# Turning queries and keys inside the first projection instead of in a stage behind it

## The chip, the cores and the metric

The kernel runs on one core of one Trainium2 chip. The metric is the device time of one execution in microseconds (us); lower is better. The median of several executions is compared. The profile is one execution more, recorded by the hardware profiler.

## The reference

Two blocks of a network on 512 tokens of 1024 features, all in float32. The part that matters here is the start of the first block. 16 meta tokens are put ahead of the 512, so there are 528 positions; the rows are normalised and multiplied by `w_in`:

```python
proj = jnp.einsum('btd,dc->btc', a, w_in)
aq, ak, av, rq, rf, ri, rg = jnp.split(proj, SPLIT_POINTS, axis=-1)

def apply_rope(z, cos, sin):
    half = z.shape[-1] // 2
    rot = jnp.concatenate([-z[..., half:], z[..., :half]], axis=-1)
    return (z * cos.astype(z.dtype) + rot * sin.astype(z.dtype)).astype(z.dtype)
```

`apply_rope` is the turning by position of the queries `aq` and the keys `ak`, before the attention's scores. Each of the seven parts of `proj` has 512 columns. The second block needs a modulation vector, `mod = silu(c) @ w_ada + b_ada`, a product of one row with a 1024 x 9216 matrix; it doesn't depend on the first block, and the kernel does it beside the first projection. Behind all this come a gated scan, a layer of 16384 experts, and the second block.

## The kernel before

The code is written for each engine by hand, in blocks. All engines meet at a barrier at the end of a block, and within one they are ordered by semaphores alone. Every engine runs its own instructions strictly in order, so what stands behind a waiting instruction waits too.

**Loading** (`load_first`) fetches the tokens and small tables. **Normalising** (`norm_to_features`) makes the features, split in a high and a low part so that three fast products stand for one in float32.

**The first projection** (`first_projection`, which calls `project`) goes over 28 weight slabs of 512 KB. Slabs 0 to 15 give features: slab b holds 128 columns of the weights, and its result `t.fm[:, b, :]` (128 x 528) is made in two halves of 264, each in a PSUM bank. Blocks 0 to 3 are the queries, 4 to 7 the keys. Slabs 16 to 27 are "wide": three groups of four slabs, each group adding up five (the last group four) outputs of 128 x 512. The way of a slab:

- SP loads it into `proj_raw`, three deep, when `proj_w_low` of the slab three before is done.
- ACT rounds it to `proj_w_high` (two deep) when PE has finished the slab two before. Then ACT moves the finished outputs from PSUM.
- DVE makes `proj_w_low`, the rest (`split_low`, L408).
- PE multiplies (L149 to L151), 48 matmuls for a slab of features, 30 or 24 for a wide one. Outputs go round eight banks.

After each `split_low` DVE calls `beside_dve`: the modulation. `w_ada` comes in 96 pieces of 128 x 768 (384 KB), fetched by POOL into the ring `ada`, four deep (L563). DVE multiplies a piece by its column of c and adds it to `ada_acc` (L579). A slab has four pieces, so slabs 24 to 27 have none. POOL first clears `ada_acc` (L556) and loads the bias (L558), and behind the 96 pieces it fetches the three tables of the rotation.

**The rotation** (`rotate_first`) is a block of its own. For each of the eight feature blocks of queries and keys PE multiplies by the matrix `turn` (which swaps and negates the halves) into a bank pair (L607), DVE multiplies that by `sin` into `swung` (L616), multiplies `t.fm` by `cos` (L618) and adds the two (L620). Two bank pairs and two `swung` buffers alternate.

**Attention** (`first_attention`) needs all that, and the causal `mask`, which SP loads at the start of the rotation block. Its scores are L676, the addition of the mask L745. The gated scan behind it is the first to read `ada_acc`.

Of the kernel before, what the change touches and what calls it, by code (L numbers as in the profile page):

```python
# [18 lines left out]
ALU = mybir.AluOpType  # L19
# [3 lines left out]
P = 128  # L23
D = 1024
# [4 lines left out]
NT = NM + T  # L29
HALF = NT // 2  # L30
BANK = 512
# [5 lines left out]
AH, AHD, AV = 4, 64, 128  # L37
# [75 lines left out]
def sbuf(nc, ctx, name, shape, dtype=F32):  # L113
    return ctx.enter_context(nc.sbuf_tensor(numbered(name), shape, dtype))
# [15 lines left out]
def psum(nc, ctx, name, shape):  # L130
    return ctx.enter_context(nc.psum_tensor(numbered(name), shape, F32))
# [147 lines left out]
def load_first(core, t, dram):  # L279

    nc = core.nc
    with ExitStack() as ctx:
# [6 lines left out]
        dots, exps = core.sem("small_dots"), core.sem("small_exps")  # L289
        block = ctx.enter_context(nc.Block(no_gpsimd_drain=True))  # L290
        n_loads = 12
        c_in = core.sem("c_in")

        @block.sync
        def _(sp):
            sp.dma_start(t.c_col[:, :], dram["c_2"]).then_inc(c_in, 16)
            sp.dma_start(t.meta[:, :], dram["meta_tokens"]).then_inc(loaded, 16)
            sp.dma_start(t.x[:, :, :], dram["x"].rearrange("o (t p) d -> p (o t) d", p=P)).then_inc(loaded, 16)
            sp.dma_start(t.ident[:, :], dram["ident"]).then_inc(loaded, 16)
            sp.dma_start(t.mix_norm[:, :], dram["mix_norm_w"]).then_inc(loaded, 16)  # L300
            sp.dma_start(t.ffn_norm[:, :], dram["ffn_norm_cols"]).then_inc(loaded, 16)
            sp.dma_start(lb_in[:, :, :], dram["rec_lb_logits"]).then_inc(loaded, 16)
            for n, name in enumerate(("diff_lambda_q1", "diff_lambda_k1", "diff_lambda_q2", "diff_lambda_k2")):
                sp.dma_start(lam_in[:, n, :], dram[name].broadcast_to([P, AHD])).then_inc(loaded, 16)
            sp.dma_start(t.mixed_scale[:, 0:AH], dram["diff_subln_w"]).then_inc(loaded, 16)
            sp.dma_start(t.mixed_scale[:, AH:AH + RH], dram["rec_norm_w"]).then_inc(loaded, 16)

        @block.vector
        def _(dve):
# [126 lines left out]
            s.used(self.n)  # L436


def project(core, feat, weights, moves, beside=None, beside_dve=None, before_moves=None, beside_act=None):

    nc = core.nc
    BANKS = 8
    slabs = weights.slabs
    N = len(slabs)
    with ExitStack() as ctx:
# [11 lines left out]
        def _(pe):  # L461
            for n, slab in enumerate(slabs):
                pe.wait_ge(low.handle, low.at(n + 1))
                hi, lo = weights.parts(n)
                for (at, count), e in zip(slab.ranges, slab.outs):
# [14 lines left out]
                    if e == slab.outs[-1]:  # L480
                        last.then_inc(used.handle, 1)
                    elif closes:
                        last.then_inc(out_done.handle, 1)


        @block.scalar
# [53 lines left out]

def first_projection(core, t, dram, feat, weights, moves, rope):

    ACH, DEEP = 768, 4
    PARTS, PER_SLAB = 9 * D // ACH, 4
    with ExitStack() as ctx:
        ada = sbuf(core.nc, ctx, "ada", [P, DEEP, ACH])
        ada_in = [core.sem(f"ada_in{i}") for i in range(DEEP)]
        ada_used, acc_clear, acc_bias = core.sem("ada_used"), core.sem("acc_clear"), core.sem("acc_bias")
        N = PARTS * KC
        assert N <= PER_SLAB * weights.n  # L550

        def beside(block):
            @block.gpsimd
            def _(pool):

                pool.memset(t.ada_acc[:, :], 0.0).then_inc(acc_clear, 1)  # L556
                pool.wait_ge(acc_clear, 1)
                pool.dma_start(t.ada_acc[0:1, :], dram["b_ada_2"]).then_inc(acc_bias, 16)  # L558
                for n in range(N):
                    if n >= DEEP:  # L560
                        pool.wait_ge(ada_used, n - DEEP + 1)
                    k, part = n // PARTS, n % PARTS
                    pool.dma_start(ada[:, n % DEEP, :], dram["w_ada_2"][0, k * P:(k + 1) * P, part * ACH:(part + 1) * ACH])\  # L563
                        .then_inc(ada_in[n % DEEP], 16)
                pool.dma_start(rope.turn[:, :], dram["rope_turn"]).then_inc(rope.tables, 16)
                pool.dma_start(rope.cos[:, :], dram["rope_cos"]).then_inc(rope.tables, 16)
                pool.dma_start(rope.sin[:, :], dram["rope_sin"]).then_inc(rope.tables, 16)

        def beside_dve(dve, slab, moved):

            for n in range(PER_SLAB * slab, min(N, PER_SLAB * (slab + 1))):
                if n == 0:
                    dve.wait_ge(acc_bias, 16)
                k, part = n // PARTS, n % PARTS
# [4 lines left out]
                dve.scalar_tensor_tensor(acc, ada[:, n % DEEP, :], t.c_col[:, k:k + 1], acc, ALU.mult, ALU.add)\  # L579
                   .then_inc(ada_used, 1)  # L580

        project(core, feat, weights, moves, beside, beside_dve)


def rotate_first(core, t, dram, rope):

    nc = core.nc
    with ExitStack() as ctx:
        turn, cos, sin, tables = rope.turn, rope.cos, rope.sin, rope.tables
        swung = sbuf(nc, ctx, "swung", [P, 2, NT])  # L590
        bank = [psum(nc, ctx, f"rot_bank{i}", [P, 2, BANK]) for i in range(2)]
        turned, swung_done = [core.sem(f"rope_{n}") for n in ("turned", "swung")]
        mask_in = core.sem("mask_in")
        block = ctx.enter_context(nc.Block(no_gpsimd_drain=True))

        @block.sync
        def _(sp):
            sp.dma_start(t.mask[:, :], dram["causal"]).then_inc(mask_in, 16)

        @block.tensor  # L600
        def _(pe):
            pe.wait_ge(tables, 48)
            for b in range(2 * AH):
                if b >= 2:
                    pe.wait_ge(swung_done, b - 1)
                for half in range(2):
                    last = pe.matmul(bank[b % 2][:, half, 0:HALF], turn[:, :], t.fm[:, b, half * HALF:(half + 1) * HALF],  # L607
                                     start=True, stop=True)
                last.then_inc(turned, 1)

        @block.vector
        def _(dve):
            chain = core.chain(dve, "dve_step")
            for b in range(2 * AH):
                dve.wait_ge(turned, b + 1)
                dve.tensor_tensor(swung[:, b % 2, :].rearrange("p (a n) -> p a n", a=2), bank[b % 2][:, :, 0:HALF],  # L616
                                  sin[:, :].rearrange("p (a n) -> p a n", a=2), ALU.mult).then_inc(swung_done, 1)
                chain.link(dve.tensor_tensor(t.fm[:, b, :], t.fm[:, b, :], cos[:, :], ALU.mult))  # L618
                dve.wait_ge(swung_done, b + 1)
                chain.link(dve.tensor_tensor(t.fm[:, b, :], t.fm[:, b, :], swung[:, b % 2, :], ALU.add))  # L620


def first_attention(core, t, dram):
# [10 lines left out]
    with ExitStack() as ctx:  # L634
# [23 lines left out]
        def long(u):  # L658
            return units[u][1] == TT - 1

        def meta_turned(u):
            return over[0:NM, 2, :] if long(u) else turn_bank[0:NM, units[u][1] + 1, :]

        @block.tensor
        def _(pe):
# [2235 lines left out]
def build(nc, dram, out):  # L2901
    NAMES.clear()
    LIMIT = 229344
    with ExitStack() as ctx:
# [10 lines left out]
        with ExitStack() as first:  # L2915
# [31 lines left out]
            behind = nc.sbuf_base  # L2947
            with ExitStack() as turned:
                t.mask = sbuf(nc, turned, "mask", [P, P])
                rotate_first(core, t, dram, rope)  # L2950
                first_attention(core, t, dram)
            gated_scan(core, t, dram)

# [158 lines left out]
```

## Time and profile before

| | |
|---|---|
| median of 3 runs | 3123.35 us (3122.04 to 3127.35) |
| the profiled execution | 3135.32 us |
| its span, first to last instruction | 3133.5 us |
| mean granted TensorE clock | 0.935 of 2.4 GHz |
| PE, DVE, ACT, POOL busy | 86%, 61%, 41%, 21% |
| projection, in the trace | 38.9 to about 233 us |
| rotation, in the trace | 233.3 to 252 us |

The stages follow one another, so a share over the whole span says little of the first 8% of it. The views used are the groups of instructions, the timelines of single engines, and busy time by window. PE is the matmul engine (PEld its weight loads), DVE the vector engine, ACT the scalar engine, POOL and SP issue DMAs. An arrow in square brackets names what ended the idle time before an instruction. "DMA to landing" is the time from issue to the semaphore.

### The profile page before, as it was taken

Reading aid. Unit: us, or ns where it says so; the run is one execution under the profiler, and the core shown is the slowest. Engines: PE = TensorE matmul, PEld = TensorE weight load, DVE = VectorE, ACT = ScalarE, POOL = GpSimd, SP = SyncE. Lnnn points to the kernel's source line nnn. Section 1 sums busy time; section 2 is a strip of 40 time slices with the busy share of each in tenths; the row PEclk is TensorE's granted clock in tenths of the full one; section 3 lists DMA queues with packets and bytes.
Section 4 is the critical chain, followed back from the end, with each engine's and each line's share of the span. In section 5 each row is a group of like instructions: output and inputs, shape, how many; then the busy total and the mean of one; then the engine's idle time right before and its main releaser. Section 6 shows DMA issues by size and latency. Waiting matters only on the chain. (4 is left out here: it accounts for less than half of the span.)

```text
span 3133.5 us, 32433 instructions
## 1 busy us (share of the span) xinstructions
PE 2688.3 (86%) x11370; PEld 1823.2 (58%) x11370; DVE 1898.3 (61%) x3882; ACT 1276.2 (41%) x2760; POOL 662.1 (21%) x638
## 2 busy tenths in 40 slices
PE   5997778797889877789999998898998886889997
PEld 5974657343444322255555554697784355778886
DVE  5757745777777677777777776554645544433323
ACT  2223423444444444555666654443243254222221
POOL 2310000444443444434444434000000100000000
PEclk8996689999999999999999999899996898999999
DMA  5950014999999999999999999454220001222321
GB/s 182 328 201 1 1 54 128 373 412 405 420 420 421 408 412 421 418 411 414 419 415 414 413 418 410 155 183 141 88 69 3 36 1 61 74 94 95 101 100 61
DMA packets 131107, 750.80 MB, mean 240 GB/s; under 512 B 17296, under 2 KB 17824, under 8 KB 64624
## 3 DMA queue, kind: packets, MB, share of 16 engines
q0 software_dynamic: 81824, 575.43, 45.1%
q1 hardware_dynamic: 49120, 173.30, 15.9%
q8 instruction: 90, 1.47, 0.2%
q14 instruction: 73, 0.60, 0.1%
HBM read 746.57 MB, written 2.10 MB: 239 GB/s over the span
## 5 line engine op out<-in xcount | busy, mean ns | idle before, releaser
L1566 PE MATMUL peer_y<-rows,diag 128*128 128x512 f32 x2048 | 995.6, 613 | 176.6 <-ACT diag L1546 165.8
L1520 DVE CUSTOM_DVE_ANT_0 rows<-rows,hidden 128x1024 f32<-128x1024 f32 x512 | 627.5, 1226 | 374.0 <-DMA rows<-in_peer_table,experts 367.3
L1507 POOL DMA_INDIRECT rows<-in_peer_table,experts x512 | 582.2, 1137 | 1046.2 <-PE peer_y L1566 799.2
L1566 PEld LDWEIGHTS peer_y<-rows,diag 128*128 128x128 f32 x2048 | 362.4, 192 | 592.4 <-ACT diag L1546 302.9
L1543 ACT ACTIVATE hid<-hid 128x1 f32<-128x1 f32 x512 | 102.7, 201 | 542.2 <-DVE hid L1520 533.0
L2020 DVE TENSOR_TENSOR piece_w_low<-piece_raw,piece_w_high 128x1024 fp32r<-128x1024 f32 x132 | 160.9, 1223 | 102.2 <-ACT piece_w_high L2015 102.2
L1546 ACT ACTIVATE diag<-ident,hid 128x128 f32<-128x128 f32 x512 | 205.6, 402 | 16.7
L2015 ACT ACTIVATE piece_w_high<-piece_raw 128x1024 fp32r<-128x1024 f32 x132 | 138.6, 1052 | 109.3 <-PE u_bank L151 77.6
L2142 DVE TENSOR_TENSOR silu<-silu,u_bank 128x256 f32<-128x256 f32 (+1 forms) x44 | 24.4, 555 | 229.1 <-PE u_bank L151 229.1
L402 ACT ACTIVATE proj_w_high<-proj_raw 128x1024 fp32r<-128x1024 f32 (+2 forms) x57 | 57.7, 1014 | 245.8 <-PE proj_bank L151 245.7
L1544 ACT ACTIVATE hid<-hid,gates 128x1 f32<-128x1 f32 x512 | 150.8, 295 | 16.6
L149 PE MATMUL peer_y<-peer_feat_high,early_w_high 128*128 128x256 f32 x352 | 144.3, 410 | 1.8 <-issue 1.8
L149 PE MATMUL query_bank<-half_feat_high,query_w_high 128*128 128x256 f32 x256 | 116.3, 454 | 15.0 <-DVE query_w_low L408 15.0
L579 DVE SCALAR_TENSOR_TENSOR ada_acc<-ada,c_col,ada_acc 128x768 f32<-128x768 f32 x96 | 95.1, 1018 | 42.1 <-DMA ada<-in_w_ada 41.6
L408 DVE TENSOR_TENSOR proj_w_low<-proj_raw,proj_w_high 128x1024 fp32r<-128x1024 f32 (+2 forms) x57 | 66.1, 1166 | 78.9 <-ACT proj_w_high L402 78.8
L151 PE MATMUL peer_y<-peer_feat_high,early_w_low 128*128 128x256 f32 x352 | 98.8, 281 | 0.0
L150 PE MATMUL peer_y<-peer_feat_low,early_w_high 128*128 128x256 f32 x352 | 98.8, 281 | 0.0
L149 PE MATMUL proj_bank<-feat_high,proj_w_high 128*128 128x264 f32 x256 | 75.5, 295 | 20.2 <-DVE proj_w_low L408 13.9
L149 PEld LDWEIGHTS peer_y<-peer_feat_high,early_w_high 128*128 128x128 f32 x352 | 66.8, 190 | 30.8 <-issue 29.8
L2130 ACT ACTIVATE act_t_high<-silu 128x256 fp32r<-128x256 f32 (+1 forms) x44 | 23.2, 526 | 148.9 <-DVE silu L2142 148.9
L150 PEld LDWEIGHTS peer_y<-peer_feat_low,early_w_high 128*128 128x128 f32 x352 | 66.7, 189 | 28.0 <-issue 27.1
L1779 DVE TENSOR_TENSOR early_w_low<-early_raw,early_w_high 128x1024 fp32r<-128x1024 f32 x66 | 80.6, 1222 | 1.1
(502 smaller groups left out, 5842.8 us busy)
## 6 DMA issues: line engine op xcount, KB each, us to landing
ada<-in_w_ada POOLq DMA_DIRECT2D x96, 384.0 KB, 4.8
piece_raw<-in_ffn_w_gate SPq DMA_DIRECT2D x44, 512.0 KB, 3.5
piece_raw<-in_ffn_w_up SPq DMA_DIRECT2D x44, 512.0 KB, 4.4
piece_raw<-in_ffn_w_down SPq DMA_DIRECT2D x44, 512.0 KB, 3.5
query_raw<-in_peer_w_query SPq DMA_DIRECT2D x32, 512.0 KB, 6.2
early_raw<-in_ffn_w_gate SPq DMA_DIRECT2D x22, 512.0 KB
early_raw<-in_ffn_w_up SPq DMA_DIRECT2D x22, 512.0 KB
early_raw<-in_ffn_w_down SPq DMA_DIRECT2D x22, 512.0 KB
```

The source lines that it names most:

```text
L149: pe.matmul(out, left[0], right[0], start=start, stop=False)
L150: pe.matmul(out, left[0], right[1], start=False, stop=False)
L151: return pe.matmul(out, left[1], right[0], start=False, stop=stop)
L579: dve.scalar_tensor_tensor(acc, ada[:, n % DEEP, :], t.c_col[:, k:k + 1], acc, ALU.mult, ALU.add)\
L1507: pool.indirect_dma_start(self.rows[:, b, :], None, self.table, bass.IndirectOffsetOnAxis(ap=self.experts[:, unit % self.SETS, n % TOPK:n ...
L1520: dve.tensor_tensor_reduce(out=self.rows[:, b, 0:D], in0=self.rows[:, b, 0:D], in1=self.hidden[:, tile, :], scale=1.0, scalar=0.0, op0=ALU ...
L1543: chain.link(act.activation(self.hid[:, 1, b:b + 1], self.hid[:, 0, b:b + 1], ACT.Gelu))
L1544: chain.link(act.activation(self.hid[:, 2, b:b + 1], self.hid[:, 1, b:b + 1], ACT.Copy, scale=self.gates[:, unit % self.SETS, n % TOPK:n % ...
L1546: act.activation(self.diag[:, b, :], self.t.ident[:, :], ACT.Copy, scale=self.hid[:, 2, b:b + 1])\
L1566: last = pe.matmul(self.y[self.bank(tile)][:, c * BANK:(c + 1) * BANK], self.diag[:, b, :], self.rows[:, b, D + c * BANK:D + (c + 1) * BAN ...
L2015: act.activation(self.w.high[:, p % self.RING, :], self.raw[:, p % self.RING, :], ACT.Copy)\
L2020: dve.tensor_tensor(self.w.low[:, p % self.RING, :], self.raw[:, p % self.RING, :], self.w.high[:, p % self.RING, :].bitcast(F32), ALU.sub ...
```

## The change

The rotation stage goes. Its PE part moves into PE's projection loop by a new hook, `beside_pe`: behind slabs 3, 6, 9, ..., 24 PE turns block 0, 1, 2, ..., 7. Its DVE part moves into `beside_dve` of the slab behind: after that slab's `split_low` and ahead of its modulation pieces. There is one bank pair and one `swung`, so the projection's outputs go round six banks instead of eight. The `ada` ring is three deep instead of four. The 96 pieces are dealt out over all 28 slabs (three or four in each) instead of four in each of the first 24. The rotation's tables are fetched behind the third piece. Clearing `ada_acc` and loading the bias move into the loading block, and the load of the mask moves to the start of attention.

```diff
@@ load_first
+        acc_clear, acc_bias = core.sem("acc_clear"), core.sem("acc_bias")
...
+        @block.gpsimd
+        def _(pool):
+            pool.memset(t.ada_acc[:, :], 0.0).then_inc(acc_clear, 1)
+            pool.wait_ge(acc_clear, 1)
+            pool.dma_start(t.ada_acc[0:1, :], dram["b_ada_2"]).then_inc(acc_bias, 16)
@@ project
-    BANKS = 8
+    BANKS = banks_used
...
+                if beside_pe is not None:
+                    beside_pe(pe, n, moved)
@@ first_projection
-    ACH, DEEP = 768, 4
-    PARTS, PER_SLAB = 9 * D // ACH, 4
+    ACH, DEEP = 768, 3
+    TURN_AT = {3 * b + 3: b for b in range(2 * AH)}
+    PARTS = 9 * D // ACH
...
-                pool.memset(t.ada_acc[:, :], 0.0).then_inc(acc_clear, 1)
-                pool.wait_ge(acc_clear, 1)
-                pool.dma_start(t.ada_acc[0:1, :], dram["b_ada_2"]).then_inc(acc_bias, 16)
                 for n in range(N):
+                    if n == DEEP:
+                        pool.dma_start(rope.turn[:, :], dram["rope_turn"]).then_inc(rope.tables, 16)
+                        pool.dma_start(rope.cos[:, :], dram["rope_cos"]).then_inc(rope.tables, 16)
+                        pool.dma_start(rope.sin[:, :], dram["rope_sin"]).then_inc(rope.tables, 16)
...
+        def beside_pe(pe, slab, moved):
+            if slab in TURN_AT:
+                b = TURN_AT[slab]
+                pe.wait_ge(moved.handle, moved.at(2 * b + 2))
+                if b == 0:
+                    pe.wait_ge(rope.tables, 48)
+                else:
+                    pe.wait_ge(swung_done, b)
+                for half in range(2):
+                    last = pe.matmul(turn_bank[:, half, 0:HALF], rope.turn[:, :], t.fm[:, b, half * HALF:(half + 1) * HALF],
+                                     start=True, stop=True)
+                last.then_inc(turned, 1)
 
         def beside_dve(dve, slab, moved):
-            for n in range(PER_SLAB * slab, min(N, PER_SLAB * (slab + 1))):
+            if slab - 1 in TURN_AT:
+                chain = core.chain(dve, "dve_step")
+                b = TURN_AT[slab - 1]
+                dve.wait_ge(turned, b + 1)
+                dve.tensor_tensor(swung[:, :].rearrange("p (a n) -> p a n", a=2), turn_bank[:, :, 0:HALF],
+                                  rope.sin[:, :].rearrange("p (a n) -> p a n", a=2), ALU.mult).then_inc(swung_done, 1)
+                chain.link(dve.tensor_tensor(t.fm[:, b, :], t.fm[:, b, :], rope.cos[:, :], ALU.mult))
+                dve.wait_ge(swung_done, b + 1)
+                chain.link(dve.tensor_tensor(t.fm[:, b, :], t.fm[:, b, :], swung[:, :], ALU.add))
+
+            for n in range(N * slab // weights.n, N * (slab + 1) // weights.n):
...
-        project(core, feat, weights, moves, beside, beside_dve)
+        project(core, feat, weights, moves, beside, beside_dve, beside_pe=beside_pe, banks_used=6)
-def rotate_first(core, t, dram, rope):
...
@@ first_attention
+        @block.sync
+        def _(sp):
+            sp.dma_start(t.mask[:, :], dram["causal"]).then_inc(mask_in, 16)
@@ build
-                rotate_first(core, t, dram, rope)
```

## Rows read from the trace of the kernel before

**Rows 1.** Groups of instructions, 0 to 300 us: count, busy and mean, idle before and releaser.

```profile
L579 DVE SCALAR_TENSOR_TENSOR ada_acc<-ada,c_col,ada_acc 128x768 f32<-128x768 f32 x96 | 95.1, 1018 | 42.1 <-DMA ada<-in_w_ada 41.6
L149 PE MATMUL proj_bank<-feat_high,proj_w_high 128*128 128x264 f32 x256 | 75.5, 295 | 20.2 <-DVE proj_w_low L408 13.9 <-PEq L164 6.3
```

**Rows 2.** Windows: length, then busy PE, PEld, DVE, ACT, POOL; clock, DMA share, GB/s.

```profile
135.00:152.00 17.00, 17.00 (x141) 16.94 (x139) 13.57 (x14) 4.58 (x9) 5.95 (x12) 1.00 0.98 346
...
233.00:253.00 20.00, 10.99 (x37) 7.40 (x39) 16.25 (x24) 0.69 (x1) 0.00 (x0) 0.86 0.01 3
```

**Rows 3.** ACT's timeline in the projection: start, duration, operation.

```profile
52.67 1.06 ACT L402 ACTIVATE proj_w_high<-proj_raw 128x1024 fp32r<-128x1024 f32 x1 [4.22 <-PE proj_bank L151]
...
76.20 1.06 ACT L402 ACTIVATE proj_w_high<-proj_raw 128x1024 fp32r<-128x1024 f32 x1 [4.25 <-PE proj_bank L151]
...
146.42 1.06 ACT L402 ACTIVATE proj_w_high<-proj_raw 128x1024 fp32r<-128x1024 f32 x1 [4.23 <-PE proj_bank L151]
...
152.27 1.06 ACT L402 ACTIVATE proj_w_high<-proj_raw 128x1024 fp32r<-128x1024 f32 x1 [4.22 <-PE proj_bank L151]
...
167.10 1.06 ACT L402 ACTIVATE proj_w_high<-proj_raw 128x1024 fp32r<-128x1024 f32 x1 [5.86 <-PE proj_bank L151]
174.03 1.06 ACT L402 ACTIVATE proj_w_high<-proj_raw 128x1024 fp32r<-128x1024 f32 x1 [5.87 <-PE proj_bank L151]
...
181.91 2.04 ACT L502 ACTIVATE tm<-proj_bank 128x512 f32<-128x512 f32 x4
...
214.21 1.06 ACT L402 ACTIVATE proj_w_high<-proj_raw 128x1024 fp32r<-128x1024 f32 x1 [2.11 <-PE proj_bank L151]
219.78 1.06 ACT L402 ACTIVATE proj_w_high<-proj_raw 128x1024 fp32r<-128x1024 f32 x1 [4.51 <-PE proj_bank L151]
```

**Rows 4.** DVE's timeline: end of loading, third slab, one period of a later slab.

```profile
14.87 0.17 DVE L329 TENSOR_SCALAR one_lb<-lb 128x4 f32<-128x4 f32 x1
...
60.91 1.22 DVE L408 TENSOR_TENSOR proj_w_low<-proj_raw,proj_w_high 128x1024 fp32r<-128x1024 f32 x1
...
94.98 2.88 DVE L579 SCALAR_TENSOR_TENSOR ada_acc<-ada,c_col,ada_acc 128x768 f32<-128x768 f32 x3
99.95 1.02 DVE L579 SCALAR_TENSOR_TENSOR ada_acc<-ada,c_col,ada_acc 128x768 f32<-128x768 f32 x1 [2.09 <-DMA ada<-in_w_ada]
```

**Rows 5.** POOL's timeline: the memset, the first four pieces, one later piece.

```profile
38.92 7.79 POOL L556 MEMSET ada_acc<- 128x9216 f32 x1 [38.47 <-POOLq L164]
...
47.67 2.17 POOL L563 DMA_DIRECT2D ada<-in_w_ada  x4
...
96.29 0.54 POOL L563 DMA_DIRECT2D ada<-in_w_ada  x1 [1.53 <-DVE ada_acc L579]
```

**Rows 6.** Timeline from the rotation's start to attention's start, all engines.

```profile
233.30 5.72 PE L607 MATMUL rot_bank<-fm,turn 128*128 128x264 f32 x16 [2.52 <-PEq L449]
...
239.96 1.16 PE L607 MATMUL rot_bank<-fm,turn 128*128 128x264 f32 x4 [0.94 <-DVE swung L616]
...
241.30 0.71 DVE L616 TENSOR_TENSOR swung<-rot_bank,sin 128x528 f32<-128x528 f32 x1
...
252.36 1.76 PE L676 MATMUL score<-fm 64*128 64x144 f32 x8 [4.94 <-PEq L588]
253.65 0.30 DVE L745 TENSOR_TENSOR score<-score,mask 128x128 f32<-128x128 f32 x1 [1.89 <-PE score L676]
```

**Rows 7.** Landing times: `ada` over all, `ada` issued at 47 to 50 us, `mask`.

```profile
DMA to landing us min/median/max: 3.4/4.8/6.4
...
DMA to landing us min/median/max: 3.7/4.3/5.0
...
DMA to landing us min/median/max: 1.7/1.7/1.7
```

**Rows 8.** Two windows of slab 2; the third figure from the end is the clock.

```profile
62.00:65.00 3.00, 2.81 (x13) 2.82 (x14) 2.84 (x4) 0.00 (x0) 1.00 (x2) 0.50 0.96 328
...
67.00:69.00 2.00, 2.00 (x19) 2.00 (x18) 1.25 (x2) 0.00 (x0) 0.00 (x0) 1.00 0.98 375
```

More of the change, by code:

```diff
@@ L436, in close, with project @@
             s.used(self.n)
-def project(core, feat, weights, moves, beside=None, beside_dve=None, before_moves=None, beside_act=None):
+def project(core, feat, weights, moves, beside=None, beside_dve=None, before_moves=None, beside_act=None, beside_pe=None,
+            banks_used=8):
     nc = core.nc
-    BANKS = 8
+    BANKS = banks_used
     slabs = weights.slabs
@@ L541, in first_projection @@
 def first_projection(core, t, dram, feat, weights, moves, rope):
-    ACH, DEEP = 768, 4
-    PARTS, PER_SLAB = 9 * D // ACH, 4
+    ACH, DEEP = 768, 3
+    TURN_AT = {3 * b + 3: b for b in range(2 * AH)}
+    PARTS = 9 * D // ACH
     with ExitStack() as ctx:
         ada = sbuf(core.nc, ctx, "ada", [P, DEEP, ACH])
+        swung = sbuf(core.nc, ctx, "swung", [P, NT])
+        turn_bank = psum(core.nc, ctx, "rot_bank", [P, 2, BANK])
         ada_in = [core.sem(f"ada_in{i}") for i in range(DEEP)]
-        ada_used, acc_clear, acc_bias = core.sem("ada_used"), core.sem("acc_clear"), core.sem("acc_bias")
+        turned, swung_done = core.sem("rope_turned"), core.sem("rope_swung")
+        ada_used, acc_bias = core.sem("ada_used"), core.sem("acc_bias")
         N = PARTS * KC
-        assert N <= PER_SLAB * weights.n
         def beside(block):
@@ L564, in _ @@
                         .then_inc(ada_in[n % DEEP], 16)
-                pool.dma_start(rope.turn[:, :], dram["rope_turn"]).then_inc(rope.tables, 16)
-                pool.dma_start(rope.cos[:, :], dram["rope_cos"]).then_inc(rope.tables, 16)
-                pool.dma_start(rope.sin[:, :], dram["rope_sin"]).then_inc(rope.tables, 16)
-        def beside_dve(dve, slab, moved):
-            for n in range(PER_SLAB * slab, min(N, PER_SLAB * (slab + 1))):
+        def beside_pe(pe, slab, moved):
[10 more added lines that the diff above has]
+                last.then_inc(turned, 1)
+        def beside_dve(dve, slab, moved):
+            if slab - 1 in TURN_AT:
[8 more added lines that the diff above has]
+            for n in range(N * slab // weights.n, N * (slab + 1) // weights.n):
                 if n == 0:
@@ L580, in beside_dve @@
                    .then_inc(ada_used, 1)
-        project(core, feat, weights, moves, beside, beside_dve)
-def rotate_first(core, t, dram, rope):
[L587 to L620, printed above, removed]
+        project(core, feat, weights, moves, beside, beside_dve, beside_pe=beside_pe, banks_used=6)
 def first_attention(core, t, dram):
```

## The prediction

> **What bounds the kernel now.** I read the page first: PE is busy for 86% of the span and DVE for 61%, and the tenths show that the stages follow one another, each with a bound of its own. Nearly all the edits lie in the first 253 us, so I asked for groups of instructions, for the timeline of each engine, and for windows of that stretch. It holds the projection (28 weight slabs, 38.9 to 231 us) and the rotation (233 to 252 us). Blocks of code end at a barrier, so what is won or lost before attention moves everything behind it by the same amount, and only this stretch needs a sum.
>
> The groups say that PE's matmuls of the projection waited 13.9 us for `proj_w_low`, and that DVE's modulation pieces waited 41.6 us for their own DMAs [rows 1]. Read them together: the engine that stands still is PE, the one that holds it is DVE, and DVE is held by the ring of `ada` buffers. The windows show how near that DMA path is to full: 0.98 of the DMA time at 346 GB/s while PE and DVE both work, and against it a rotation stage in which DVE works for 16.25 of 20 us and PE for 11 [rows 2].
>
> ACT's timeline gives the pace, since each `proj_w_high` starts when PE has finished a slab. A 264-column slab takes 5.85 us where PE is free (146.42 to 152.27), a slab of five outputs 6.93 us, one of four outputs 5.57 us; but slabs 3 to 15, from 76.20 to 152.27, took 76.1 us, not 12 x 5.85 = 70.2 [rows 3]. So DVE's pace costs 5.9 us there. One period on DVE shows why: three pieces run back to back in 2.88 us, the fourth waits 2.1 us for its DMA, and only then comes the next `proj_w_low` [rows 4]. Before that, the first modulation piece can't be fetched until a memset of 7.79 us and the bias are through on POOL [rows 5]; DVE must do eight pieces before the third `proj_w_low`, which starts at 60.91 [rows 4].
>
> **The change, part by part.** I count from the profiled execution, 3135.32 us with a span of 3133.5 us.
>
> *Rotation stage removed.* From its first matmul at 233.30 to the first of attention at 252.36: 19.06 us [rows 6]. This gain is certain, and the question is what is paid back inside the projection.
>
> *Memset and bias moved into loading.* POOL had stood idle for 38.47 us before the memset [rows 5]; loading ends on DVE at 15.04 [rows 4], so 7.8 us are hidden there, and if they weren't, at most 7.8 us would come back. The pieces now start at 38.9 instead of 47.67. DVE owes six pieces, not eight, before the third `proj_w_low`. Hand count: 38.9 + 3.7 landing [rows 7] + about 1.5 for two slab loads issued at the same time = 44; first use 1 us, reissue 0.3, landing 4.3, some 1.75 us of the three rope tables queued ahead of piece 3 (0.6 MB at the 346 GB/s of [rows 2]), three more pieces 2.9: 54.3, up to 56 with the tables' own issue, where 60.91 was. Slab 3 then ends 5 us earlier. Bounds: 3.5 and 8 (PE's wait gone altogether). I take 5.0.
>
> *Eight turns put into PE's queue.* Each is two calls, four records: 1.16 us of busy PE with a pipelined tail [rows 6], about 1.04 us until the next slab can start. 8 x 1.04 = 8.3 us. What waits behind the turn on PE is the next slab. The waits of the turn itself (`moved`, `swung_done`, tables) are for work two or more slabs old and cost nothing.
>
> *Rotation on DVE.* The first operation started 1.34 us after PE's (239.96 to 241.30) [rows 6]; three operations of about 0.7 us. Counted from PE's release of the turn, 0.3 + 2.0 = 2.3 us. DVE now **waits for PE** here: behind that wait stand the slab's modulation pieces and the next `proj_w_low`, and PE waits for that. After the turn PE has one slab (5.85 us) of work. In that time DVE must do 2.3 us of rotation, the pieces, and 1.2 us of `proj_w_low`.
> With three pieces, all landed: 2.3 + 2.9 + 1.2 = 6.4, a stall of 0.55 us.
> With four pieces, the fourth must be fetched into a buffer that the first has just left, because the ring is now three deep. The trip is use 0.96 (three in 2.88) + reissue 0.29 (the piece begun at 94.98 ends at 96.00, POOL issues at 96.29 [rows 4, 5]) + landing. Landing is 3.7 to 4.3 where little is under way and 4.8 in the median now [rows 7]; with fewer pieces in flight I take 3.7 to 4.3, a trip of 5.0 to 5.5. Then 2.3 + 5.0 + 0.96 + 1.2 = 9.5 (to 10.0), a stall of 3.6 to 4.2 us.
> The even dealing gives 3, 3, 4, 3, 4, 3, 4 pieces and repeats. Turning slabs with four are 4, 13, 16 and 25. Stalls: 3.6 to 4.2 twice, 2.5 to 3.1 before slab 17 (PE has 6.93), 3.9 to 4.5 before slab 26 (PE has 5.57), 0.55 twice, none at 19 and 22. Sum 14.7 to 17.1 us.
>
> *Ring between turns.* DVE's cycle of three slabs is 2.3 + 3.43 x 5.0 to 5.5 = 19.5 to 21.2 us; PE's with its turn is 18.6, and with the mean stall above 20.8. So 0 to 0.8 us more in each of four cycles, 0 to 3; I take 1.5. In exchange the 5.9 us of today's pace are gone, since the turning cycles replace it.
>
> *Six banks.* At slabs 20 and 24 the second output needs a bank that ACT moves only after its `proj_w_high`. The first of four moves (2.04 us) is over 0.6 us after 181.91. ACT saw the slab's end at 174.03 + 6.93 = 180.96, PE had it some 0.4 us before and gets to the second output, 1.4 us of matmuls later, at about 181.9 [rows 3]. 0.6 us twice, 1.2; with slower moves up to 2.
>
> *Pieces in slabs 24 to 27.* These had none; now about 14. They hide behind PE's 5.57 us per slab (3.4 x 0.96 + 1.2 = 4.5), except for the stall already counted. If DVE ended after PE, the surplus would show behind the last slab.
>
> *Mask.* Now fetched as attention begins. It lands 1.7 us after issue [rows 7]; DVE's first operation came 1.29 us after PE's first (252.36 to 253.65) [rows 6]: +0.4 us. Attention starts right behind a busy PE, at the full clock for a moment, which I put at 0.5 us gained (bounds 0 and 2).
>
> **Sum.** -19.06 - 5.0 + 8.3 + 15.9 + 1.5 - 5.9 + 1.2 + 0.4 - 0.5 = -3.2. With the clock (below) one time in three 2 us: -2.5. Forecast 3132.8 us for the profiled execution; the median 3123.35 is 12 us lower, and I take the same difference from it: 3120.9 us. About 0.2% (6.2 us) is what a measurement can tell from no change, so the likeliest case is "within".
>
> **Where a rule speaks.** The trace lands a piece of 384 KB in 3.4 us at best and 4.8 in the median [rows 7]. The Trainium skill, "DMA: Bandwidth & Descriptors", on the fixed cost of a DMA, fits 2.0 us plus bytes over 436 GB/s, an estimate of 2.9 us for such a piece; by it the four long stalls would be some 1.1 us shorter each and the sum near -8. No row here shows so short a landing.
> PE had slab 1 behind it before 52.67 [rows 3] and waited until the third `proj_w_low` was done at 62.1 [rows 4]; then it ran at 0.50 and was at 1.00 again by 67 us [rows 8]: 1.2 GHz for about 4.4 us (an estimate), a loss of 2.2 us. The rotation stage, with gaps of 0.94 us between its turns [rows 6] and 4 us of idle PE at its end, had a mean of 0.86 [rows 2]. The new gaps of 2.5 to 4.5 us lie between. The Trainium skill, "TensorE: Matmul & The Clock Gate", on HAM oscillation, warns that DMA waits between groups of matmuls bring the lower clock again and again; by it, each long stall costs 2.2 us more, the sum becomes +5 or so, still within.
>
> **Rivals.**
> *Faster.* The ring of three suffices: landing comes down far enough, or DVE arrives with more slack than I count, and the four long stalls shrink to 0.55. Then 14.7 becomes about 3.5 and the ring term is 0: -3.2 - 12.4 - 1.5 = -17, 3106 us. For it: DMA is at 0.98 now, and demand falls from 4 to 3.43 pieces in a slab. Against it: a lone landing is still 3.4 to 3.7 us, so the fourth piece is late. It decides (over 6.2 us) once two of the four stalls are gone. Half of it gives -9.
> *Slower.* Landing stays at today's 5.0 us because weight slabs share the path. Then the trip is 6.25 us and a turn cycle lasts 2.3 + 3.43 x 6.25 = 23.7 us: 2.5 more than the 21.2 of above in each of four cycles, 1 more in the three over wide slabs (3 x 6.93 + 1.04 and a mean stall of 0.9 make 22.7). +13, net +10.5, 3134 us. It decides (over +6.2) from a landing of about 4.7. For it: 0.98 busy DMAs. Against it: most of that landing is queueing among four pieces.
> *Within.* The sum as it stands, with the clock rule or without.
>
> **Chances.** Within 0.2%: 0.42. Faster: 0.36 (full rival 0.12, part of the stalls missing 0.24). Slower: 0.22 (landing 0.14, clock plus landing 0.08). The range reaches into both: 3107 (the full rival less its tail) to 3136 (the slower rival's centre and 2 us of lower clock). The likeliest case alone spans 3117 to 3129.
>
> **What would show it.** No rotation stage, attention's first matmul near 250 us. `proj_w_low` of slab 2 starts at 54 to 56. In slabs 4, 13, 16 and 25 DVE waits once for an `ada` DMA behind three pieces, and PE waits 2.5 to 4.5 us for `proj_w_low` after it; elsewhere under 1 us. PE's waits in the projection sum to 17 to 25 us. `ada` lands in 3.7 to 4.3 us. POOL's memset lies before 10 us. It would be wrong if the waits stand in other slabs, if the median landing is 3.4 or 5, or if PE's clock falls in the gaps.

## The result, and the profile after

The change makes the kernel slightly slower: 3131.6 us in the median of 20 runs (3124.05 to 3139.91) against 3125.62 us (20 runs, 3121.5 to 3136.13), a ratio of 1.0021, interval 1.0013 to 1.0029. The forecast was 2.5 us less, 3120.9 us, with "within 0.2%" as the likeliest case and a range of 3107 to 3136. The time lies in the range but beyond the 3117 to 3129 of the likeliest case, and it moved the other way: 6.0 us more, at the edge of 0.2% (0.19% by the medians, 0.21% by the ratio).

The profiled execution alone would mislead. Its span is 3131.0 us, 2.5 us under the one before. So I split each span at attention's first vector operation, which closes the stretch that the change touches.

The timeline of the changed kernel there, the same lines as [rows 6]:

```profile
253.56 2.06 ACT L512 ACTIVATE tm_gate<-proj_bank 128x512 f32<-128x512 f32 x4 [16.58 <-PE proj_bank L151]
...
255.99 1.76 PE L676 MATMUL score<-fm 64*128 64x144 f32 x8 [2.51 <-PEq L457]
...
259.67 0.30 DVE L745 TENSOR_TENSOR score<-score,mask 128x128 f32<-128x128 f32 x1 [9.41 <-DMA mask<-in_causal]
```

The vector operation stood at 253.65 before [rows 6] and stands at 259.67 now: +6.0 us, which is also the difference of the medians. That they agree so exactly is luck: in a second trace of the changed kernel (c2, below) it stands at 261.04. The rest took 3133.5 - 253.65 = 2879.9 us in the profile before and 3131.0 - 259.67 = 2871.3 us in the one after; no edit reaches it, and over the traces of this study it lies between 2867.3 and 2879.9. All comparisons of traces below are therefore made up to that operation.

The last moves of the projection (`tm_gate`) began at 230.87 before, 253.56 now. That is 22.7 us more, where 19.06 are saved. ACT's timeline says where, to be read as [rows 3]: each line comes when PE has finished a slab, here slabs 2 to 6, 13 to 17, 25.

```profile
64.16 1.06 ACT L409 ACTIVATE proj_w_high<-proj_raw 128x1024 fp32r<-128x1024 f32 x1 [8.98 <-PE proj_bank L151]
70.28 1.06 ACT L409 ACTIVATE proj_w_high<-proj_raw 128x1024 fp32r<-128x1024 f32 x1 [4.51 <-PE proj_bank L151]
77.04 1.06 ACT L409 ACTIVATE proj_w_high<-proj_raw 128x1024 fp32r<-128x1024 f32 x1 [5.14 <-PE proj_bank L151]
87.94 1.06 ACT L409 ACTIVATE proj_w_high<-proj_raw 128x1024 fp32r<-128x1024 f32 x1 [9.28 <-PE proj_bank L151]
93.79 1.06 ACT L409 ACTIVATE proj_w_high<-proj_raw 128x1024 fp32r<-128x1024 f32 x1 [4.23 <-PE proj_bank L151]
...
142.99 1.06 ACT L409 ACTIVATE proj_w_high<-proj_raw 128x1024 fp32r<-128x1024 f32 x1 [5.14 <-PE proj_bank L151]
153.97 1.06 ACT L409 ACTIVATE proj_w_high<-proj_raw 128x1024 fp32r<-128x1024 f32 x1 [9.36 <-PE proj_bank L151]
159.82 1.06 ACT L409 ACTIVATE proj_w_high<-proj_raw 128x1024 fp32r<-128x1024 f32 x1 [4.23 <-PE proj_bank L151]
167.65 1.06 ACT L409 ACTIVATE proj_w_high<-proj_raw 128x1024 fp32r<-128x1024 f32 x1 [6.22 <-PE proj_bank L151]
178.66 1.06 ACT L409 ACTIVATE proj_w_high<-proj_raw 128x1024 fp32r<-128x1024 f32 x1 [9.95 <-PE proj_bank L151]
...
235.93 1.06 ACT L409 ACTIVATE proj_w_high<-proj_raw 128x1024 fp32r<-128x1024 f32 x1 [5.40 <-PE proj_bank L151]
```

Slab 5 took 10.90 us, slab 14 took 10.98, slab 17 took 11.01, and the last two together 17.63: with 5.85, 5.85, 6.93 and 11.1 for the same slabs where nothing holds PE, 5.1 + 5.1 + 4.1 + 6.5 = 20.8 us too long. These are the four places that the prediction names. The turn costs less than estimated: slab 4, behind a turn, took 6.76, so 0.9 us.

DVE's timeline around the first of them, as [rows 4]:

```profile
67.61 1.22 DVE L415 TENSOR_TENSOR proj_w_low<-proj_raw,proj_w_high 128x1024 fp32r<-128x1024 f32 x1
71.09 0.71 DVE L599 TENSOR_TENSOR swung<-rot_bank,sin 128x528 f32<-128x528 f32 x1 [2.26 <-PE rot_bank L590]
...
73.19 2.88 DVE L613 SCALAR_TENSOR_TENSOR ada_acc<-ada,c_col,ada_acc 128x768 f32<-128x768 f32 x3
77.95 1.02 DVE L613 SCALAR_TENSOR_TENSOR ada_acc<-ada,c_col,ada_acc 128x768 f32<-128x768 f32 x1 [1.88 <-DMA ada<-in_w_ada]
78.89 1.22 DVE L415 TENSOR_TENSOR proj_w_low<-proj_raw,proj_w_high 128x1024 fp32r<-128x1024 f32 x1
```

DVE stands 2.26 us for PE, rotates, does three landed pieces, waits 1.88 us for the fourth, and then makes `proj_w_low`, done at 80.1. ACT saw slab 4's end at 77.04, so PE had run out of work by then. And what PE does when the work comes, in the windows behind two of the gaps (columns as [rows 2]):

```profile
78.00:80.00 2.00, 0.00 (x0) 0.00 (x0) 2.00 (x2) 0.66 (x3) 0.54 (x1) 1.00 0.70 261
80.00:82.00 2.00, 1.84 (x12) 1.84 (x13) 1.96 (x3) 0.00 (x0) 0.54 (x1) 0.84 0.66 169
82.00:84.00 2.00, 2.00 (x12) 2.00 (x11) 1.12 (x2) 0.00 (x0) 0.54 (x1) 0.50 1.01 395
84.00:86.00 2.00, 2.00 (x15) 2.00 (x15) 1.03 (x1) 0.00 (x0) 0.54 (x1) 0.81 1.05 333
...
240.00:242.00 2.00, 2.00 (x6) 1.56 (x5) 1.27 (x2) 0.00 (x0) 0.97 (x2) 0.50 0.58 187
242.00:244.00 2.00, 2.00 (x6) 1.52 (x6) 1.88 (x2) 0.00 (x0) 0.64 (x2) 0.50 0.87 280
```

The first four windows belong to the gap before slab 5, the last two to the one before slab 26. The clock falls to 0.50 (1.2 GHz) behind the gap; the lost shares of the first four add up to 3.4 us at 0.50. The four gaps themselves, as PE's timeline has them:

```profile
80.16 0.39 PE L149 MATMUL proj_bank<-feat_high,proj_w_high 128*128 128x264 f32 x1 [3.24 <-DVE proj_w_low L415]
...
146.21 0.59 PE L149 MATMUL proj_bank<-feat_high,proj_w_high 128*128 128x264 f32 x1 [3.33 <-DVE proj_w_low L415]
...
169.77 0.54 PE L149 MATMUL proj_bank<-proj_w_high,feat_high 128*128 128x512 f32 x1 [2.24 <-DVE proj_w_low L415]
...
239.46 0.79 PE L149 MATMUL proj_bank<-proj_w_high,feat_high 128*128 128x512 f32 x1 [3.66 <-DVE proj_w_low L415]
```

3.24, 3.33, 2.24 and 3.66 us, where 3.6 to 4.2 twice, 2.5 to 3.1 and 3.9 to 4.5 were predicted; and the windows behind the second and third also show the lower clock (0.56 from 147 to 150, 0.52 from 170 to 172). In finer windows the trace has 3.4 us at 0.50 behind each of the first three gaps and 6.8 behind the fourth, 5.7 of them with PE at work. Half of these 16.0 us is lost, an estimate of 8.0 us. With the gaps, 12.5 us together, that makes 20.5 of the 20.8 us above. The chain of waits from 38 to 262 us:

```profile
DVE ada_acc L613 <- DMA ada<-in_w_ada: 51.7, 43, 7.7
PEld proj_bank L149 <- DVE proj_w_low L415: 24.3, 13, 4.1
PE proj_bank L149 <- DVE proj_w_low L415: 20.7, 11, 3.7
DVE swung L599 <- PE rot_bank L590: 18.6, 7, 4.3
```

PE waited 20.7 us in total, inside the 17 to 25 of the prediction, and at most 3.7 at once. "Elsewhere under 1 us" did not hold before slab 12: 1.89 us there, behind a slab of four pieces that follows a turning one.

### The profile page after: what moved, and what is told of

The parts are those of the page before. It is cut to its first block and busy times, and to the rows that moved or that the text cites. A ratio compares the mean times of both kernels' runs of the same rounds, so it can differ in the third digit from the quotient of the medians.

```text
span 3131.0 us, 32420 instructions
## 1 busy us (share of the span) xinstructions
PE 2688.1 (86%) x11370; PEld 1824.3 (58%) x11370; DVE 1901.4 (61%) x3882; ACT 1276.6 (41%) x2760; POOL 667.7 (21%) x638
## 5 line engine op out<-in xcount | busy, mean ns | idle before, releaser
L579 POOL DMA_DIRECT2D ada<-in_w_ada x96 | 51.7, 539 | 183.3 <-DVE ada_acc L613 152.8
```

## The experiments

Four kernels undo or cure one part of the changed kernel, two take parts of it alone onto the kernel before, two combine the cures, one deals the pieces differently, and one repeats. Projection times are the start of the last ACT moves minus the start of the first `proj_w_high` of ACT in it, because the first 47 us vary from trace to trace by up to 1.6 us (46.15 to 47.72): 184.0 before, 205.8 after.

**a1: the rotation behind the pieces on DVE.**

```diff
@@ beside_dve
-            if slab - 1 in TURN_AT:
-                ...
             for n in range(N * slab // weights.n, N * (slab + 1) // weights.n):
...
+            if slab - 1 in TURN_AT:
+                ...
```

> The changed kernel, with one thing moved: on DVE the rotation of a block stands behind the slab's modulation pieces instead of ahead of them. Theory 1 (DVE stands behind PE, then owes too much before the next proj_w_low, and PE's clock falls in the gap that follows): while DVE waits for the turn it now does the pieces, and after the turn it owes only 2.3 us of rotation and 1.2 us of proj_w_low, under PE's 5.85 us. The four long stalls (14 us together), the short ones and the lower clock (2.2 us each) go; attention's first vector operation comes at 235 to 240 us instead of 259.7, and the kernel takes 20 us less than the changed one, 14 us less than the one before (ratio 0.995 to 0.996). Theory 2 (the cost is PE's own added matmuls, the six banks, or the fuller DMA path): these are all still there, so the first vector operation of attention stays at 255 us or later and the ratio above 1.000.

3117.22 us, ratio 0.9968 (0.9955 to 0.9981); attention's first vector operation at 246.60, projection 193.9 us. Faster than before and 14 us less than the changed kernel, as theory 1 has it and against theory 2; but short of the 20 us that it claimed (13 of 20 to 25 in the trace). Its trace still has a gap of 2.31 us before slab 5, with the clock at 0.50 behind it, and one of 2.84 us before slab 14, behind which the clock stayed at 1.00. DVE at the first:

```profile
75.39 1.02 DVE L603 SCALAR_TENSOR_TENSOR ada_acc<-ada,c_col,ada_acc 128x768 f32<-128x768 f32 x1 [0.85 <-DMA ada<-in_w_ada]
76.33 0.70 DVE L610 TENSOR_TENSOR swung<-rot_bank,sin 128x528 f32<-128x528 f32 x1
...
78.42 1.22 DVE L415 TENSOR_TENSOR proj_w_low<-proj_raw,proj_w_high 128x1024 fp32r<-128x1024 f32 x1
```

DVE no longer stands for PE, but the fourth piece of a ring of three is still late, and the rotation now comes after it. The order on DVE is a part of the cause.

**a2: PE kept at work in the gaps.** The matmuls added write nothing that is read.

```diff
         def beside_pe(pe, slab, moved):
+            if slab - 1 in TURN_AT and slab in (4, 13, 16, 25):
+                pe.wait_ge(swung_done, TURN_AT[slab - 1] + 1)
+                for _ in range(6):
+                    pe.matmul(turn_bank[:, 0, 0:HALF], rope.turn[:, :], rope.cos[:, 0:HALF], start=True, stop=True)
```

> The changed kernel, with PE kept at work in the four long gaps: behind slabs 4, 13, 16 and 25 it multiplies a table by a table six times (about 3 us) into the bank pair of the rotation, a result that nobody reads. DVE's work is unchanged. If the clock is a cost of its own, the gaps stay as long (PE's next slab starts when it did) but the slab behind each runs at full clock: granted clock 1.00 in the windows behind the gaps, 4 x 2.2 us less, minus up to 0.5 us each where the added work outlasts the gap: attention's first vector operation at 251 to 254 us instead of 259.7, ratio about 0.999 to 1.000. If instead DVE's lateness alone sets the pace (the slow slab would only eat slack), nothing changes or it gets 1 to 2 us longer: 259 to 262 us.

3125.25 us, ratio 0.9991 (0.9982 to 1.0001), 6.4 us under the changed kernel. Projection 199.5 us instead of 205.8. DVE does the same; PE does 24 useless products and is done sooner. The windows behind the gaps:

```profile
80.00:84.00 4.00, 3.71 (x30) 3.71 (x31) 3.01 (x4) 0.00 (x0) 1.07 (x2) 1.00 0.85 273
...
146.00:150.00 4.00, 4.00 (x35) 4.00 (x35) 2.94 (x3) 0.00 (x0) 1.61 (x3) 1.00 0.97 383
170.00:174.00 4.00, 4.00 (x19) 3.23 (x19) 3.77 (x4) 0.00 (x0) 1.07 (x2) 1.00 0.97 336
...
239.00:243.00 4.00, 4.00 (x19) 3.25 (x18) 3.04 (x4) 0.00 (x0) 0.76 (x2) 1.00 0.77 195
```

1.00 in all four. So the clock is a cost of its own, 6.3 us net; the projection without the added products took 208.7 us in c2 and 205.5 in a4. The falls that are gone had cost 8.0 us (the estimate above), but this trace has a new one: before slab 12, where nothing was added, PE waited 2.15 us, and the clock was at 0.50 from 128 to 131 us. Slab 12 took 9.81 us instead of 7.98.

**a3: the ring four deep.**

```diff
-    ACH, DEEP = 768, 3
+    ACH, DEEP = 768, 4
...
-        swung = sbuf(core.nc, ctx, "swung", [P, NT])
+        swung = Scratch(core.nc, t.meta_at, t.meta_at + 4 * D).sbuf("swung", [P, NT])
```

> The changed kernel, with the ring of modulation pieces four deep as before (the buffer swung moved onto the dead rows of meta to make room). Theory 1, with the ring as the cause: four landed pieces at a turn cost 2.3 + 3.9 + 1.2 = 7.4 us, a stall of 1.5 instead of 3.6 to 4.2, too short for the clock to fall: 4 x 2.2 + 4 x 2.2 = 17 us less than the changed kernel, attention's first vector operation at 241 to 245 us, ratio 0.996 to 0.998. Rival (the order on DVE alone is the cause, or the DMA path is full): the fourth piece is still late, DVE's wait of 1.9 us behind three pieces stays, and the gain is under 5 us.

3109.45 us, ratio 0.995 (0.9933 to 0.9966). Projection 184.8 us, 21 less than with three buffers, and attention's first vector operation at 235.13. More than expected, and the rival is out. At the first turn four pieces now run through, and `proj_w_low` follows 5.8 us behind the start of the rotation instead of 7.8, PE's gap is 1.29 us, and its clock stays at 1.00 there, as it does from 59 to 232 us (no gap in that stretch is over 1.6 us):

```profile
68.70 0.71 DVE L599 TENSOR_TENSOR swung<-rot_bank,sin 128x528 f32<-128x528 f32 x1 [2.87 <-PE rot_bank L590]
...
70.80 3.81 DVE L613 SCALAR_TENSOR_TENSOR ada_acc<-ada,c_col,ada_acc 128x768 f32<-128x768 f32 x4
74.52 1.22 DVE L415 TENSOR_TENSOR proj_w_low<-proj_raw,proj_w_high 128x1024 fp32r<-128x1024 f32 x1
```

**a4: the mask fetched with the rotation's tables.**

```diff
                         pool.dma_start(rope.sin[:, :], dram["rope_sin"]).then_inc(rope.tables, 16)
+                        pool.dma_start(t.mask[:, :], dram["causal"]).then_inc(core.sem("mask_in"), 16)
@@ first_attention
-        @block.sync
-        def _(sp):
-            sp.dma_start(t.mask[:, :], dram["causal"]).then_inc(mask_in, 16)
```

> The changed kernel, with the mask fetched behind the rotation's tables in the projection, as a fourth table, instead of at the start of attention. If the mask's 3.7 us of landing are what attention waits for, its first vector operation comes 1.0 to 1.4 us behind PE's first matmul instead of 3.7, so 2.4 us less; projection unchanged within 1 us. If not (something else would end last), less than 0.5 us. By the clock of executions 2.4 us is 0.08%, under what the timing can tell; the trace decides.

3130.93 us, ratio 1.0017 (1.0005 to 1.0029). The vector operation comes 0.6 us behind PE's first, which now runs at the full clock (0.97 us for eight records, where the changed kernel took 1.76):

```profile
254.10 0.97 PE L673 MATMUL score<-fm 64*128 64x144 f32 x8 [2.51 <-PEq L457]
254.70 0.30 DVE L742 TENSOR_TENSOR score<-score,mask 128x128 f32<-128x128 f32 x1 [6.29 <-PE score L673]
```

In the changed kernel it came 3.7 us behind, so 3.1 us are gone. The times alone couldn't show it: the interval holds the 1.0021 of the changed kernel.

**b1: memset and bias moved, nothing else, on the kernel before.**

```diff
@@ load_first
+        @block.gpsimd
+        def _(pool):
+            pool.memset(t.ada_acc[:, :], 0.0).then_inc(acc_clear, 1)
...
@@ first_projection
-                pool.memset(t.ada_acc[:, :], 0.0).then_inc(acc_clear, 1)
...
```

> The kernel before, with only the memset of ada_acc and the bias load moved into the loading block. By the step of the prediction (pieces fetched 8.75 us earlier, 5 us gained, less than 8.75 because eight pieces are still owed before the third proj_w_low): that proj_w_low starts at 55 to 57 us instead of 60.9, PE's longest wait falls from 9.6 to 4 to 5 us, the projection's last ACT moves start 4 to 5 us earlier than at 230.9. If the move costs something in loading (the changed kernel started its projection 0.7 us later), the gain is 3 to 4 us. Ratio 0.998 to 0.999.

3122.35 us, ratio 0.9983 (0.9974 to 0.9992). The last moves begin at 225.67 instead of 230.87, 5.2 us earlier, and attention's vector operation at 248.89, 4.8 earlier. The third `proj_w_low` starts at 55.00, and PE's longest wait is 3.6 us, less than the 4 to 5 expected. The step of 5.0 us is right.

**b2: the same, and the ring three deep with even dealing; rotation in its own stage.**

```diff
-    ACH, DEEP = 768, 4
+    ACH, DEEP = 768, 3
...
-            for n in range(PER_SLAB * slab, min(N, PER_SLAB * (slab + 1))):
+            for n in range(N * slab // weights.n, N * (slab + 1) // weights.n):
```

> The kernel of b1_memset_only with the ring three deep and the pieces dealt out evenly over 28 slabs, and the rotation left in its own stage. Theory 1 (a short ring is dear only together with the turn, because DVE stands for PE while the ring stands full, and then owes four pieces at once): 3.43 pieces per slab at 5.0 to 5.3 us per three are 5.7 to 6.1 us, about PE's 5.85, so the projection ends within 3 us of b1's, before or after. Rival (a ring of three is dear by itself): slabs 3 to 15 take over 80 us, as against 76.1 before, and the projection ends over 5 us later than b1's.

3123.61 us, ratio 0.9989 (0.9979 to 0.9999); last moves at 226.46 against b1's 225.67. Slabs 4 to 15 took 79.6 us against 76.3 in b1, 3.4 more, most of it given back elsewhere. So the ring of three with the even deal costs 0.8 us without the turns; with the turns, under the same deal, the ring alone costs 21 (a3). The two figures are not quite alike, since b2 changes the deal too, from four pieces in a slab to 3.43, and no run has the short ring with the old deal. The reason fits the lines at the first turn, but no run isolates it: while DVE stands for PE the ring is full and fetches nothing, and those fetches are owed afterwards.

**b3 and b4: the cures together.** b3 is the changed kernel with the edits of a1 and a3 and an early mask (on the dead rows of `meta`). b4 deals the pieces over slabs 1 to 27:

```diff
-            for n in range(N * slab // weights.n, N * (slab + 1) // weights.n):
+            for n in range(max(0, N * (slab - 1) // (weights.n - 1)), N * slab // (weights.n - 1)):
```

> The changed kernel with a ring four deep (swung on the dead rows of meta), the rotation behind the pieces on DVE, and the mask fetched behind the rotation's tables. If order and ring cure the same stalls, the order adds little to the ring alone: 0 to 4 us less than a3_deep4 in the projection, and 0.7 us from the mask: attention's first vector operation at 230 to 234 us instead of 235.1; ratio 0.993 to 0.995. If the order adds its own 15 us on top, 220 us; if it undoes something (a turn's result taken later, so the next turn or the next slab's proj_w_low waits), over 236.

> b3_best with the pieces dealt out over slabs 1 to 27 instead of 0 to 27, so that DVE owes three, not six, before the third proj_w_low. PE's wait before slab 2 was the longest left (about 5 us in the changed kernel, with the lower clock behind it). If that wait is DVE's debt of pieces: proj_w_low of slab 2 starts at 49 to 51 us, PE waits under 1 us, clock 1.00 in slab 2, and everything comes 4 to 6 us earlier than in b3_best. If it's the later slabs' pieces that bind (3.56 a slab instead of 3.43), it is given back and the end is within 2 us of b3_best.

b3: 3099.08 us, ratio 0.9911 (0.9898 to 0.9924). b4: 3097.96 us, ratio 0.9903 (0.9888 to 0.9919). These are the fastest kernels here. The waits of PE, b3 first, then b4:

```profile
PE proj_bank L149 <- DVE proj_w_low L415: 2.7, 1, 2.7
```

```profile
PE proj_bank L149 <- DVE proj_w_low L415: 0.6, 1, 0.6
```

b3's vector operation stands at 227.26, under the expected 230 to 234: order and ring cure partly different waits (the order another 6.7 us of projection, 184.8 to 178.1). b4's is at 224.38, 2.9 us earlier, less than the 4 to 6 expected. Its slab 2 takes 4.5 us less (5.85 instead of 10.34), but slab 5 takes 0.8 more, and b3's trace began its projection 0.6 us sooner. Between b3 and b4 the times don't decide; the traces do by the wait that is gone.

**c1: three pieces in every slab with a rotation, ring still three deep.**

```diff
-            for n in range(N * slab // weights.n, N * (slab + 1) // weights.n):
+            for n in range(DEAL[slab], DEAL[slab + 1]):
```

> The changed kernel, ring three deep and rotation ahead of the pieces, but the 96 pieces dealt out so that each of the eight slabs with a rotation has three (72 in the other 20, three or four each; the first three slabs as in the changed kernel). Theory 1, the fourth piece: at a turn DVE owes 2.3 + 2.9 + 1.2 = 6.4 us, so the four gaps of about 3.5 us become 0.6 (wide slabs: none) and PE's clock stays at 1.00. Gain 4 x 3 + 4 x 2.2 = 20 us, less what the fuller slabs between cost (3.6 pieces at 1.7 us are 6.1 us, up to 0.5 over PE's pace in 20 slabs): the last ACT moves at 236 to 244 us instead of 253.6. Rival (any wait of DVE for PE with a short ring costs, whatever the deal): the gaps only move to the slabs between, and the moves come at 249 us or later.

3125.27 us, ratio 0.9996 (0.9985 to 1.0007); projection 200.5 us, so 5.3 of the 20 us. The last moves begin at 246.63, between the 244 of theory 1 and the 249 of the rival. In part the gap has moved one slab on. Slabs 5 and 6 of c1:

```profile
83.11 1.06 ACT L409 ACTIVATE proj_w_high<-proj_raw 128x1024 fp32r<-128x1024 f32 x1 [4.84 <-PE proj_bank L151]
...
93.74 1.06 ACT L409 ACTIVATE proj_w_high<-proj_raw 128x1024 fp32r<-128x1024 f32 x1 [9.02 <-PE proj_bank L151]
```

Slab 5 is cured (6.46 us), and slab 6 takes 10.63, with the clock at 0.51 from 86 to 88 us. PE's gap before slab 6 is 2.97 us. Slab 9 took 10.57 in the same way. PE's gaps of 2 us and more stand before slabs 6, 9 and 15. This deal gives slabs 5, 8 and 14 four pieces and slab 11 three, and before slab 12 PE lost little (it took 6.22 us). So the fourth piece still decides; it only has to come soon behind a turn, not in the turning slab. In b2, without turns, the gaps behind slabs of four were 2.3 us at most, so the turn has a share in it.

**c2: the changed kernel once more.**

> The changed kernel once more. If the four long gaps, PE's lower clock behind them and the late mask belong to it, they're in this trace too: PE's gaps in the same slabs, last ACT moves 251 to 254 us, the mask landing in over 3 us. If the clock's fall or the mask's 3.7 us were chance, they come out otherwise: fewer falls of the clock, or a mask at 1.7 us as before. The stretch behind attention's first vector operation, which the change doesn't touch, took 2879.9 us in the profile of before and 2871.3 in that of after; if that difference is chance, this trace lies between 2866 and 2881.

One execution, 3140.62 us. Last moves at 254.91 (0.9 us behind the expected 254), vector operation at 261.04, the mask landed in 3.7 us again. Slabs 5 and 14 took 12.30 and 12.20 us, behind gaps of 3.48 and 3.38. The gap before slab 26, 3.58 us, brought the lower clock too, but the one before slab 17, 2.39 us, did not, where 2.24 us did in the other trace. A gap of 2.16 us before slab 12 brought it, as in a2, and the slab took 9.73 us. So the gaps belong to the kernel, and the fall behind those of 3.2 us and more; behind one of 2.2 to 2.4 us it may come or not. The rest took 2877.8 us, against 2871.3 in the other trace of the same kernel: that much is chance.

## Why the prediction was wrong

Summed up to attention's first vector operation, in us:

| term | predicted | measured |
|---|---|---|
| rotation stage | -19.06 | -19.1 (2.43 from last moves to scores, 21.49 before) |
| start, to the end of slab 3 | -5.0 | -5.9 (76.20 to 70.28); b1 alone 5.2 |
| eight turns on PE | +8.3 | +7.2 (0.9 each) |
| gaps, four long and two short, and ring | +17.4 | +17.2 (PE's 20.7 less some 3.5 before slab 2) |
| today's pace | -5.9 | -6.8 (154.7 from slab 3 to the last moves, 147.9 where nothing holds PE) |
| banks | +1.2 | +1.2 (0.6 at slab 20; at slab 24 0.6 in b3, where no wait for DVE hides it) |
| lower clock | +0.7 | +9.8 (what is left of 35.4 extra; 8.0 by the clock in the trace; a2 gives back 6.3) |
| mask and first matmuls | -0.1 | +2.4 |
| sum | -2.5 | +6.0 |

The 35.4 is 253.56 - 70.28 less 147.9 (12 x 5.85, 8 x 6.93 and 4 x 5.57 rounded). Of the 9.8, the 1.8 us beyond the clock's 8.0 are in no row that I can name.

**Right**, and shown: what is saved, the place and size of the gaps, the fetches of a short ring (landing 4.0 us in the median, from 4.8), the memset, the banks. The mechanism of the argument holds.

**The step that failed** is the term of the lower clock: "With the clock (below) one time in three 2 us", 0.7 us in the sum. It was too small twice over. The prediction's own price was 2.2 us for each of four long stalls, by [rows 8], so 8.8 us and a sum of "+5 or so"; a third of 8.8 would have been 2.9, but the sum took a third of 2. And the chance was too low: the clock fell behind all four of the new long gaps in one trace of the changed kernel, and in the other behind three of them and a shorter one. It cost 8.0 us by the trace, and a2 gives back 6.3. "If PE's clock falls in the gaps" was one of the prediction's signs of being wrong. It also called that case "still within"; at +6.0 us it is at the edge.

The prediction named the page "TensorE: Matmul & The Clock Gate" of the Trainium skill with the warning that such DMA waits bring the lower clock again and again. By that rule the trace agrees: 0.50 in the windows after 81 and 240 us, and with the gaps filled 1.00 (a2).

The trace of before held a nearer row than [rows 8]. The rotation's first matmul came behind a gap of 2.52 us [rows 6], and the windows there are (columns as [rows 2]):

```profile
233.00:236.00 3.00, 2.70 (x7) 2.17 (x8) 1.00 (x2) 0.00 (x0) 0.00 (x0) 0.63 0.08 22
236.00:239.00 3.00, 3.00 (x10) 1.84 (x8) 2.90 (x5) 0.00 (x0) 0.00 (x0) 0.81 0.00 0
239.00:242.00 3.00, 1.17 (x5) 0.68 (x4) 2.90 (x6) 0.00 (x0) 0.00 (x0) 1.00 0.00 0
242.00:245.00 3.00, 2.00 (x8) 1.35 (x8) 2.90 (x6) 0.00 (x0) 0.00 (x0) 1.00 0.00 0
245.00:248.00 3.00, 1.47 (x6) 0.68 (x4) 2.90 (x5) 0.00 (x0) 0.00 (x0) 1.00 0.00 0
248.00:252.30 4.30, 0.00 (x0) 0.00 (x0) 3.66 (x6) 0.00 (x0) 0.00 (x0) 0.83 0.00 0
```

So the mean of 0.86 in [rows 2], which the prediction put beside the gaps of 0.94 us between the turns, is not spread over them: between the turns the clock was 1.00, and it was lower behind the gap of 2.5 us and at the stage's idle end. A gap as short as the shortest of the predicted ones had brought the lower clock already.

**The second** is the mask, taken at its old landing of 1.7 us: it lands in 3.7 us now, and attention's first operation on DVE is 3.7 us behind PE's instead of 1.3. a4 takes 3.1 us out. And the 0.5 us for a warm start was not there: PE's first scores ran at the low clock (1.76 us for eight records, as before; in a4 0.97).

**Two slips of the working** moved nothing much. In the faster rival "14.7 becomes about 3.5" goes with a drop of 11.2, not of 12.4, which starts from the middle, 15.9; and since one stall less (over 3 us) already takes the sum from -3.2 to below -6.2, that rival would have decided with one stall gone, not two. The stretch called slabs 3 to 15 is slabs 4 to 15.

**One reason was too narrow.** The long gaps were put down to turning slabs with four pieces. In c1 those have three, and gaps of 2.97, 2.95 and 2.04 us come a slab later, behind slabs that now have four. The short ring carries the turn's delay into the next slab.

**The rivals.** The faster one (the ring suffices) did not happen: with a landing of 4.0 us in the median, 3.4 at best, the fourth piece was late. The slower one named landing at 5.0 and put the clock only beside it; the loss came by the clock at a landing of 4.0.

## What to carry to other kernels

A wait of a busy engine for another costs what stands behind it: put the work that is ready ahead of the wait. A prefetch ring can't catch up for the time in which its consumer stood still, so one that costs 0.8 us (b2, with a lighter deal) can cost 21 us once its consumer waits for something else. Where a change makes PE wait 2 to 4 us at a time, count the slow stretch behind each such gap in full, and take its chance from the gaps of that length that the trace already has. Price a moved load by what it lands in where it now stands.

## What the runs showed of the hardware

In the projections of all twelve traces, from slab 2 on, every gap of 2.9 us or more in PE's work (18 of 2.9 to 3.7 us, and one of 9.6 before) had a granted clock of 0.50 from about its end on, for 3.4 or 6.8 us (10.2 with the one of 9.6). Of twelve gaps of 2.0 to 2.9 us nine had it (2.04 in c1, 2.15 in a2, 2.16 in c2, 2.24 in after, 2.27 in a4, 2.31 in a1, 2.39 in a3, 2.71 in b3, 2.77 in b2) and three had not (2.33 in b2, 2.39 in c2, 2.84 in a1). Of those under 2.0 us (1.89 the longest, in after) none had it. The length of one gap is not the whole of it: in the rotation stage of b2 the clock was 1.00 from 231 to 241 us and fell at 241.2, where the gaps are 0.94 us each.

Six products into a bank that nobody reads, in each of four gaps, kept the clock at 1.00 there and made the kernel 6.4 us faster (a2).

The same 64 KB load by SP at the start of a block landed in 1.7 us before and in 1.8 (a3, c1), 3.0 (a2), 3.1 (a1) and 3.7 us (after, c2) in kernels with the rotation moved; no run tells why, and it stays open.

One execution's profile differs from another of the same kernel by 6.5 us in stages that the change doesn't touch (2871.3 and 2877.8, after and c2), and over all traces here by 12.6 (2867.3 to 2879.9), more than the 6 us that the change costs.
